# A two-layer mixture-of-experts decoder on one core: a fixed loop over experts, and router logits from un-normalised rows

## The reference

```python
y = hybrid_mixer(h, ...)                          # z = h @ w_in; 12 dilated heads, 4 forgetting heads
                                                  # rms norm of both groups of heads, then @ w_out
h = layer_norm(DEEPNORM_ALPHA * h + y, ln1_g, ln1_b)
logits = h @ w_router + b_router                  # 16 experts in 4 groups
probs = softmax(logits)                           # best group (by its two best), then its two best experts
gates = gv / jnp.sum(gv)                          # their probabilities, scaled to sum 1
y = sum of gate * ((silu(x @ w_gate[e]) * (x @ w_up[e])) @ w_down[e]) over the two experts e of each row
h = layer_norm(DEEPNORM_ALPHA * h + y, ln2_g, ln2_b)
```

## Time and profile before

| | us |
|---|---|
| median of 3 runs | 1367.46 |
| lowest and highest run | 1367.44, 1370.69 |
| the profiled execution, its own time | 1370.7 |
| its span | 1369.0 |
| TensorE busy with matrix products | 1122.7 |
| VectorE busy | 312.4 |
| ScalarE busy | 182.1 |

### The profile page before, as it was taken

The page is one execution under the profiler, slowest core; times in us unless marked ns, Lnnn a source line. Parts: engine busy times, 40 slices in busy tenths (PEclk is TensorE's granted clock), DMA queues, the critical chain, the costliest instruction groups (busy, mean ns, idle before and its releaser), DMA issues.

```text
span 1369.0 us, 17057 instructions
## 1 busy us (share of the span) xinstructions
PE 1122.7 (82%) x6068; PEld 571.9 (42%) x6069; DVE 312.4 (23%) x791; ACT 182.1 (13%) x373; POOL 4.6 (0%) x12
## 2 busy tenths in 40 slices
PE   7999877799977768679799975999998876577775
PEld 5776443344433233224577644445443332222232
DVE  0443531111111111112254443001111111111113
ACT  2233210001000100001223320100000100000100
POOL 0000000000000000000000000000000000000000
PEclk9999878899988899789899986999999998778888
DMA  9814319899999999999931430656989999999994
GB/s 367 360 62 164 143 44 426 350 419 428 429 428 428 429 428 429 429 428 423 419 135 62 185 143 13 246 199 264 383 326 374 429 429 428 428 428 428 428 429 204
DMA packets 34712, 444.83 MB, mean 325 GB/s; under 512 B 4080, under 2 KB 4336, under 8 KB 5872
## 3 DMA queue, kind: packets, MB, share of 16 engines
q1 hardware_dynamic: 33520, 440.08, 77.6%
q0 software_dynamic: 1152, 4.19, 0.8%
HBM read 443.22 MB, written 1.05 MB: 325 GB/s over the span
## 4 chain that ended last, share of the span: by engine, by line
PE 61%; DMA 29%; issue 6%; DVE 3%; SPq 1%; ACT 0%; DVEq 0%; ACTq 0%
DMA ring<-in_w_up_dram 23%; PE lo L566 13%; PE lo L670 9%; PE lo L554 9%; PE acc L453 8%; DMA ring<-in_w_down_dram 6%; PE acc L431 5%; PE lo L541 3%; PE acc L529 3%; PE acc L622 1%; PE lo L836 1%; PE acc L505 1%; PE lo L493 1%; PE acc L729 1%; PE lo L529 1%
## 5 line engine op out<-in xcount | busy, mean ns | idle before, releaser
L566 PE MATMUL lo<-ring,work 128*32 128x512 f32 x2112 | 276.0, 671 | 150.7 <-DMA ring<-in_w_up_dram 131.4
L566 PEld LDWEIGHTS lo<-ring,work 128*32 128x32 f32 x2112 | 68.2, 121 | 339.0 <-issue 164.0
L554 PE MATMUL lo<-ring,work 128*64 128x512 f32 x672 | 153.0, 611 | 26.4 <-issue 23.5
L541 PEld LDWEIGHTS lo<-work,h 128*128 128x128 f32 x1088 | 130.2, 193 | 53.8 <-issue 49.7
L541 PE MATMUL lo<-work,h 128*128 128x128 f32 x1088 | 146.6, 285 | 2.5 <-DVE work L1266 2.5
L670 PE MATMUL lo<-ring,work 128*128 128x512 f32 x288 | 126.8, 601 | 15.8 <-issue 15.8
L453 PE MATMUL acc<-actT,ring 128*128 128x256 f32 x512 | 119.2, 388 | 0.0
L453 PEld LDWEIGHTS acc<-actT,ring 128*128 128x128 f32 x512 | 98.6, 195 | 14.7 <-issue 1.6
L554 PEld LDWEIGHTS lo<-ring,work 128*64 128x64 f32 x672 | 48.3, 140 | 125.9 <-issue 116.6
L670 PEld LDWEIGHTS lo<-ring,work 128*128 128x128 f32 x288 | 55.2, 193 | 84.7 <-issue 84.7
L1324 DVE TENSOR_TENSOR work<-lo,work 64x512 f32<-64x512 f32 x22 | 15.0, 682 | 291.8 <-ACT work L1008 291.8
(11 more groups left out here) (183 smaller groups left out, 691.8 us busy)
## 6 DMA issues: line engine op xcount, KB each, us to landing
ring<-in_w_gate_dram SPq DMA_DIRECT2D x64, 2048.0 KB, 12.9
ring<-in_w_up_dram SPq DMA_DIRECT2D x64, 2048.0 KB, 18.7
ring<-in_w_down_dram SPq DMA_DIRECT2D x64, 2048.0 KB, 24.1
ring<-in_w_in_dram SPq DMA_DIRECT2D x24, 1024.0 KB, 25.0
ring<-in_w_out_dram SPq DMA_DIRECT2D x8, 1024.0 KB, 29.5
ln_gb<-in_ln_dram POOLq DMA_DIRECT2D x8, 512.0 KB, 7.0
cst<-in_consts_dram SPq DMA_DIRECT2D x1, 1544.0 KB, 17.9
h<-in_x_dram SPq DMA_DIRECT2D x1, 1024.0 KB, 5.2
```

Source lines behind the costliest of these rows:

```text
L541: mm = nc.tensor.matmul(lo[:, 2 + k // 4, (k % 4) * P:(k % 4 + 1) * P], h[:, t, k * P:(k + 1) * P], place_t[:, t], start=(k % 4 == 0 and t ...
L554: mm = nc.tensor.matmul(lo[half * W:(half + 1) * W, bank, :], lhsT, ring[:, s, at:at + 512], start=start, stop=stop, skip_group_check=True)
L566: return nc.tensor.matmul(lo[at * T:(at + 1) * T, bank, :], lhsT, ring[:, s, col:col + 512], start=start, stop=stop, skip_group_check=True)
```

## The change

1. **Fixed loop.** The loop over items becomes one over the 16 experts. Semaphores count in steps of 2 per expert (WHOLE); an expert with over 128 rows runs two halves inside one pass, of step 1 each. The plan (L1276 to L1305) goes; three comparisons give `kind`, and a copy of it, capped at 2, `place`. TensorE loads `kind_j` and `odd` only, and waits for `xg` after the branch. The gate table is computed after the kinds.
2. **Logits from raw rows.** With r the row before its norm, logits = (r @ (g * wr) - mean * sum(g * wr)) / std + sum(b * wr) + br. `fold_norm` makes g * wr (`wr_ln`) and the column sums once per layer during the attention, and TensorE adds the sums up over partitions in a product behind `sum_decay`. TensorE transposes `raw` instead of `h`, with `turn_raw`, and `logits` multiplies by `wr_ln`. VectorE puts the mean and the deviation in afterwards, with the sign turned round. The division by the softmax's sum goes, since ranks and gates don't need it.
3. **Order.** Block 0's product for the forgetting heads moves ahead of block 1's last dilated part, and block 0's norm stands beside it. Block 1's second product goes to the banks lo 2 and 3.
4. **Counts.** The running counts come from 2 products in place of 3, the totals apart from them (`counts_done`).

```diff
+WHOLE = 2
+DONE = WHOLE * NEXP
+TURNED = DONE + WHOLE
...
+            def turn_raw(t, banks, release=None):
+
+                for b in range(2):
+                    for i in range(4):
+                        k = 4 * b + i
+                        mm = nc.tensor.transpose(banks[b][:, i * P:(i + 1) * P], raw[:, t, k * P:(k + 1) * P], ident)
...
+            def logits(t, ks):
+
+                for k in ks:
+                    mm = nc.tensor.matmul(lo[:, 1 - t, 0:NEXP], actT[:, k, t * P:(t + 1) * P],
+                                          wr_ln[:, k, :], start=(k == 0), stop=(k == KB - 1), skip_group_check=True)
...
+                pe.wait_ge(fold_ready, l + 1)
+                nc.tensor.matmul(acc[:, 0, P + SEQ:P + SEQ + 2 * NEXP], ones, wr_sum[:].rearrange("p a e -> p (a e)"),
+                                 start=False, stop=True, skip_group_check=True).then_inc(cum_done, 1)
...
-                mix(l, 1, (2, 3), x_banks[1], 0, 5, fulls)
+                mix(l, 1, (2,), x_banks[1], 0, 5, fulls)
                 weigh_values(l, 7)
+                mix(l, 1, (3,), x_banks[1], 0, 5, fulls)
+                pe.wait_ge(sq_added, 6 * l + 6)
+                sum_squares(1)
+                pe.wait_ge(dil_taken, l + 1)
+                mix(l, 0, (6, 7), y_banks[0], 6, 7, fulls).then_inc(proj_done, 1)
                 mix(l, 1, (4, 5), x_banks[1], 0, 5, fulls).then_inc(dil_done, 1)
-                pe.wait_ge(sq_added, 6 * l + 6)
-                sum_squares(1, ring_free[ODD + 2])
-                for t in range(TB):
-                    pe.wait_ge(dil_taken, TB * l + t + 1)
-                    mix(l, t, (6, 7), y_banks[t], 6, 7, fulls).then_inc(proj_done, 1)
...
+                pe.wait_ge(raw_ready, 2 * l + 1)
+                turn_raw(0, (acc[:, 0, :], lo[:, 1, :]), ring_free[ODD + 2])
+                mix(l, 1, (6, 7), y_banks[1], 6, 7, fulls).then_inc(proj_done, 1)
+                pe.wait_ge(actT_act, 8 * l + 6)
+                logits(0, first_half)
+                pe.wait_ge(raw_ready, 2 * l + 2)
+                turn_raw(1, y_banks[1], ring_free[ODD + 3])
+                logits(0, second_half)
+                pe.wait_ge(actT_act, 8 * l + 8)
+                logits(1, range(KB))
                 for t in range(TB):
                     pe.wait_ge(h_ready, 4 * l + 3 + t)
-                    turn_block(h, t, ring_free[ODD + 3] if t == 0 else None)
...
-                mm.then_inc(logits_done, 1)
-                seed(0)
-                seed(1)
+                    seed(t)
...
-                gather(range(KB))
-                pe.wait_ge(plan_ready, l + 2)
-                n = pe.value_load(n_i[0:1, bass.ds(l, 1)], min_val=NEXP, max_val=MOST)
...
-                    expert = pe.value_load(expert_i[0:1, bass.ds(l * ITEMS + j, 1)], min_val=0, max_val=NEXP - 1)
-                    kind = pe.value_load(kind_i[0:1, bass.ds(l * ITEMS + j, 1)], min_val=0, max_val=3)
-                    odd = pe.value_load(odd_i[0:1, bass.ds(expert, 1)], min_val=0, max_val=1)
...
-                    pe.wait_ge(xg_ready, turn)
...
+                both = sel[:].rearrange("p t e -> p (t e)")
+                nc.tensor.matmul(lo[:, 0, 0:2 * NEXP], tri0[:, 0:P], both, start=True, stop=False, skip_group_check=True)
+                nc.tensor.matmul(lo[:, 0, NEXP:2 * NEXP], ones, sel[:, 0, :], start=False, stop=True,
+                                 skip_group_check=True).then_inc(ranks_done, 1)
+                for t in range(TB):
+                    mm = nc.tensor.matmul(lo[:, 1, 0:NEXP], ones, sel[:, t, :], start=(t == 0), stop=(t == 1),
+                                          skip_group_check=True)
+                mm.then_inc(counts_done, 1)
+                pe.wait_ge(place_ready, l * TURNED + WHOLE)
+                gather(range(KB), WHOLE)
+                pe.wait_ge(kinds_ready, l + 2)
+                pe.sem_inc(passed, 1)
...
+                with pe.Fori(0, NEXP) as j:
+                    done = pe.snap(l * DONE + j * WHOLE + WHOLE)
+                    turn = pe.snap(l * TURNED + j * WHOLE + WHOLE)
+                    kind_j = pe.value_load(kind_i[0:1, bass.ds(l * (NEXP + 1) + j, 1)], min_val=0, max_val=3)
+                    odd = pe.value_load(odd_i[0:1, bass.ds(j, 1)], min_val=0, max_val=1)
...
+                ln_root_of(l, 0, 0)
+                copy_turned(l, 1, 0, (acc[:, 0, :], lo[:, 1, :]))
+                copy_turned(l, 1, 1, (lo[:, 2, :], lo[:, 3, :]))
+                ln_root_of(l, 0, 1)
...
+            def fold_norm(l):
+
+                for i, scale in ((1, ln1_b), (0, ln1_g)):
+                    step(nc.vector.tensor_tensor(wr_ln[:], wr, scale.unsqueeze(2).to_broadcast([P, KB, NEXP]), ALU.mult))
+                    op = nc.vector.tensor_reduce(wr_sum[:, i, :], wr_ln[:].rearrange("p k e -> p e k"), AX.X, ALU.add)
+                    if i:
+                        step(op)
+                op.then_inc(fold_ready, 1)
...
+                y_of = (acc_tok[:, 1, :], lo_flat[:, 1024:2048])
                 for t in range(TB):
                     v.wait_ge(proj_done, 2 * l + t + 2)
-                    step(nc.vector.scalar_tensor_tensor(out=h[:, t, :], in0=acc_tok[:, 1 - t, :],
-                                                        scalar=rms[:, 2, 1, t:t + 1], in1=h[:, t, :],
-                                                        op0=ALU.mult, op1=ALU.add))
-                    layer_norm(l, 0, t, h[:, t, :])
-
-                v.wait_ge(logits_done, l + 1)
-                step(nc.vector.tensor_tensor(rt[:, 2], lo[:, 0, 0:TB * NEXP].rearrange("p (t e) -> p t e", t=TB),
-                                             br.to_broadcast([P, TB, NEXP]), ALU.add))
-                step(nc.vector.tensor_reduce(r2[:, 0], rt[:, 2], AX.X, ALU.max))
+                    nc.vector.scalar_tensor_tensor(out=raw[:, t, :], in0=y_of[t], scalar=rms[:, 2, 1, t:t + 1],
+                                                   in1=h[:, t, :], op0=ALU.mult, op1=ALU.add).then_inc(raw_ready, 1)
+                    v.wait_ge(raw_ready, 2 * l + t + 1)
+                    norm_stats(l, 0, t, raw[:, t, :])
+                    if t == 0:
+                        v.wait_ge(dil_done, 2 * l + 2)
+                        for half, bank in enumerate((acc[:, 1, :], lo[:, 0, :])):
+                            at = slice(half * 512, (half + 1) * 512)
+                            op = nc.vector.scalar_tensor_tensor(out=h[:, 1, at], in0=bank, scalar=rms[:, 2, 0, 1:2],
+                                                                in1=h[:, 1, at], op0=ALU.mult, op1=ALU.add)
+                        step(op)
+                    norm_apply(l, 0, t, raw[:, t, :])
+
+                for t in range(TB):
+                    v.wait_ge(logits_done, 2 * l + t + 1)
+                    step(nc.vector.scalar_tensor_tensor(out=rt[:, 0, t, :], in0=wr_tot[:, 0, :], scalar=mv[:, t, 0:1],
+                                                        in1=lo[:, 1 - t, 0:NEXP], op0=ALU.mult,
+                                                        op1=ALU.subtract))
+                    step(nc.vector.scalar_tensor_tensor(out=rt[:, 2, t, :], in0=rt[:, 0, t, :],
+                                                        scalar=lnt[:, 2, t:t + 1], in1=wr_tot[:, 1, :], op0=ALU.mult,
+                                                        op1=ALU.subtract))
...
+                v.wait_ge(ranks_done, l + 1)
+                step(nc.vector.tensor_tensor(rank_tab[:, :, 0:NEXP],
+                                             lo[:, 0, 0:TB * NEXP].rearrange("p (t e) -> p t e", t=TB), sel[:],
+                                             ALU.mult))
...
+                v.wait_ge(counts_done, l + 1)
...
+                nc.vector.tensor_copy(kind_i[:, bass.ds(own, NEXP)], kind[:]).then_inc(kinds_ready, 1)
```

More of the change, by code:

```diff
@@ L534, in mix, with gather @@
                 return mm
-            def gather(ks, release=None):
+            def gather(ks, n, release=None):
                 for k in ks:
@@ L672, in wide_product, with wide_gate @@
                 return mm
-            def wide_gate(last, first, gate_full, full):
+            def wide_gate(first, gate_full, full, turn, last, n):
+                pe.wait_ge(xg_ready, turn)
                 for i in range(4):
@@ L689, in wide_gate, with wide_item @@
                     mm.then_inc(ring_free[first + 3], 1)
-            def wide_item(last, full, g, turn):
+            def wide_item(full, done, next_turn, last, n):
                 for i in range(4):
@@ L720, in wide_item @@
                     if s == 3:
-                        mm.then_inc(down_done, 1)
+                        mm.then_inc(down_done, n)
                     elif last:
                         mm.then_inc(ring_free[DOWN + s], 1)
-                pe.wait_ge(placeT_ready, g + 1)
-                gather(range(4, KB), ring_free[DOWN + 3] if last else None)
-                pe.wait_ge(y_ready, g + 1)
+                pe.wait_ge(placeT_ready, done)
```

(31 more changed lines are left out.)

491 lines of the change are left out of this document (225 added, 266 removed).

## The result

The changed kernel takes 1381.43 us in the median of 4 runs (1380.6 to 1385.61), the one before 1367.45 beside it (1366.62 to 1370.69): the ratio is 1.0104, 95% interval 1.0078 to 1.013. It is 1% slower where the forecast said 1339.4 us. The profiled execution took 1381.74 us.

A forecast was written before the change was run, and what follows sets the result against it. Each layer was taken as a TensorE and VectorE chain, then a full DMA stream that can't be shortened. 2 x 9.6 + 3.9 + 4.0 + 4.6 - 0.6 - 3.0 = 28.1 us off 1367.5 gave 1339.4 us, range 1328 to 1352.

The forecast's parts named there:

- the rival of the instruction store: TensorE's expert loop outgrows its instruction store; seven other passes miss at 6.3 us each: 44 us, 1383 us; chance 0.05.
- The term for fetched instructions: TensorE's expert loop: no such term in the sum; the new loop of about 1,930 instructions was said to just fit.
- The norm and the router: Each layer ahead of the gather: shorter chain through norm, logits and ranks; gather begins 9.6 us earlier per layer.
- The path from `sel` to `place_t`: Router's end, ahead of the gather: some 2.1 us in place of 2.7, with two products ahead of the wait, not five.
- the sign "ranks begin some 13 us after block 0's last sum": Router in the changed profile: this interval was to be some 13 us, where it was 21.7.
- DMA at 0.00: Around the router: windows show idle DMA because all 16 slots are loaded and the next load waits for TensorE.
- From the gather's end to the first product: Start of each layer's expert loop: kinds written during the gather, fewer register loads; saves 3.9 and 4.0 us.
- Borders: Four gaps between passes ahead of the streams: each loses two of four register loads, 1.16 us; 4.6 us in all.
- What it adds: `fold_norm` covered during attention; its product on TensorE's path costs 0.3 us a layer: -0.6 us.
- The clock: Pause between seeds and gather may lower TensorE's clock into the gather: 1.5 us a layer charged, -3 us.

The follow-up runs named there:

- e_shared: The changed kernel, but an expert of over 128 rows runs its second half through the full pass's code (loop 1,562 instructions): 1340.39 us, 0.9804.
- the two experiments: Silu adds 1, ScalarE the other 1 ahead, so the table load precedes the wait: on e_shared 1335.3 us, on the changed kernel without the halves' code 1327.73 us.
- e_no_halves: The changed kernel without TensorE's code for experts with more than 128 rows, which no expert here takes: 1329.77 us, 0.9733.
- e_table: e_shared with the Silu of the tiny and narrow passes adding 1 and ScalarE the other 1 ahead, so the table load precedes the wait: 1335.3 us, 0.9744.

## Why the prediction was wrong

**The step that failed** is the sentence on the rival of the instruction store: "Against it: the new copies aren't visited with this data, and the visited code is as long as before." The term for fetched instructions stood at nothing in the sum. Unvisited code does count where it lies inside the loop: e_before_96 adds 97 instructions that never run to the kernel before and loses 57.7 us, and e_shared, the changed kernel with a loop of the old length, takes 1340.4 us. The rival's own size was good: 7 missed passes at 6.3 us, 44 us and 1383 us; the runs show 1381.4, and 41.0 us between it and e_shared. Its count was not: four borders miss, those around the wide passes, and at 3 to 17 us each; that seven times 6.3 gave the same is chance. What the forecast leaned on beside it, the Trainium skill ("Runtime: NRT & Kernel Launch", Instruction fetch mechanics), gives TensorE's instruction memory as 2048 instructions and says that a taken branch whose target is outside the current window of two pages forces a fetch and a stall. That a branch can stall agrees with the trace. That a loop of 1,930 fits, as the prediction took from the 2048, does not: 1,658 already misses four borders, and 1,610 none. Nor do two pages of 256 fit the traces as a window: the loop of some 1,562 before is three times as long, and its instruction packets end at 27. Here the measurement decides. With the chance of 0.05 for this case, the range of 1328 to 1352 had left it out.

**The norm and the router**, forecast 9.6 us a layer: right. The gather began 10.2 us earlier in layer 0. In layer 1 it was 30.8 us earlier, of which layer 0's end had given 19.7 (654.57 to 634.88 for block 1's statistics behind the stream): 11.1. Two slips stand in the prediction's text. The path from `sel` to `place_t` counts the 0.19 us of `sel` twice, and the sign "ranks begin some 13 us after block 0's last sum" doesn't follow from its own 154.6 and 170.8, which give 16.2; the trace shows 15.1 (155.03 to 170.13). Also, show DMA at 0.00 around the gather only; at 172 to 174 us it is 0.89.

**From the gather's end to the first product**, 3.9 and 4.0: a little small, 4.9 and 5.4 us (5.92 to 1.00 and 12.45 to 7.03). In layer 0 the plan vanished wholly, and the 1.00 us left is ScalarE's copy, near the lower bound of 0.75.

**Borders**, 4.6 us: half right. In layer 0 8.01 and 7.55 became 6.51 and 6.19, 2.9 us for 2.3. In layer 1 they are the failed step.

**What it adds**, -0.6 us: not seen apart. The change added what the forecast didn't list, the table load behind its wait, 2 to 6 us by the two experiments.

**The clock**, -3 us: wrong in sign for layer 0, right for layer 1. Layer 0's logits and gather ran at full clock, and so did the first pass's gate and up products: 7.07 us where the profile before had 10.01. So layer 0 gained up to 2.9 us where 1.5 had been charged; the profiles with layer 0 as before have 8.45 to 10.05 us there. In layer 1 the gather took 5.45 us for 3.84.

Taken together, the mechanisms that were forecast are worth about what was forecast: e_shared, where the loop is as long as before, takes 1340.4 us against the predicted 1339.4. That it is so close is luck, since it holds errors that cancel: by SyncE's issues (249.70 and 1007.70 us, 268.15 and 1037.88 in the earlier trace rows) layer 0 gave 18.5 us for the 14 of the forecast, and layer 1 11.7 for 14, with 5.5 us lost at the first wide visit. e_no_halves, whose loop is shorter than in either kernel, gains 37 us where the sum had 28.1.

## What to carry to other kernels

A loop has a length in instructions on its engine, and code in it that never runs counts too. Here 1,610 instructions cost nothing with the added code at the loop's end, and at 1,658 each change to or from the wide pass cost 7 to 21 us (3 to 17 in the changed kernel). Before adding a case to a loop, count its instructions, look whether the instruction queue's packets end after the first passes, and write the rare case so that it shares the common one's code. And look at gaps that a profile calls "issue" together with that queue's packets: together they tell a fetch from a register load.

## What was not expected of the hardware

- The step is sharp: from 1,610 to 1,658 instructions the kernel goes from 1368.2 to 1426.0 us, and at 1,931 it is no worse. What in the store makes this length the limit stays open, and so does why 48 instructions at the head cost 18.7 us and 49 at the end nothing.
- A packet of the instruction queue is 16 KB (0.84 MB in 51). In e_before_96 the 24 more of them go with 47 us of standing, 2.0 us each; in the changed kernel's pause of 16.71 us six of them begin, 2.8 us each. DMA is otherwise nearly idle then (eight packets are 2.6% of its time in 24 us), so its bandwidth isn't what TensorE waits for. Why it takes so long isn't shown.
- About 145 instructions that are never run, ahead of the loop, cost 0.5% by one border of 7.69 us in place of 1.46: where a loop begins in the program has a small price too.
- With an increment of 2 on an activation that also waits, the table load ahead of it waits too (e_shared, 516.3 us of idle time ahead of 22 loads; e_table, with increments of 1, 19.9). The load takes 1.28 us, and TensorE then waits 1.31 us in a tiny pass that isn't bound by its loads.
